# Two dense blocks in one kernel: the first stage's engine work redistributed, one chunk in plain fp32 instead of two

## The reference, cut to what matters

```
mod = silu(c) @ w_ada + b_ada            # a vector times 2048 x 12288
sh1, sc1, ... = split(mod, 6)
h = rmsnorm(x, g_pre_mix) * (1 + sc1) + sh1
proj = h @ w_in                          # 2048 x 11344: qi, qB, kB, vB, kA, vA, qA, ...
```

## Time and profile before

| what | value |
|---|---|
| median of three runs | 2582.1 us (2576.09 to 2584.29) |
| the profiled execution | 2584.16 us, its span 2582.4 us |
| TensorE matmul busy | 2546.8 us, 99% of the span |
| VectorE busy | 1732.4 us, 67% |
| ScalarE busy | 1202.8 us, 47% |
| DMA | 567.11 MB, mean 220 GB/s |
| granted TensorE clock | mean 0.995 of full |
| chain that ended last | PE 89%, DVE 7%, ACT 2%, DMA 1% |

### The profile page before, as it was taken

One profiled execution on the slowest core, in us unless ns is written; L12 is line 12 of the kernel. 1 busy time (PEld: TensorE's weight loads), 2 busy tenths in 40 slices (PEclk: granted clock), 3 DMA queues, 4 the chain that ended last, 5 costly groups with the idle time before them and its releaser, 6 DMA issues.

```text
span 2582.4 us, 30501 instructions
## 1 busy us (share of the span) xinstructions
PE 2546.8 (99%) x12354; PEld 2117.9 (82%) x12354; DVE 1732.4 (67%) x2329; ACT 1202.8 (47%) x1735; POOL 6.4 (0%) x16
## 2 busy tenths in 40 slices
PE   8999999999999999999999999999999999999998
PEld 4787788888887888888888888878788888888887
DVE  6886988788886866556556565546665575664665
ACT  4444445444446434435434465455564344443443
POOL 0000000000000000000000000000000000000000
PEclk9999999999999999999999999999999999999999
DMA  9985276588985785555555545534545555555553
GB/s 399 366 322 186 98 261 264 183 338 313 345 338 221 263 304 192 199 187 187 203 180 192 204 167 180 195 114 147 196 173 200 182 188 203 180 195 196 180 198 145
DMA packets 78748, 567.11 MB, mean 220 GB/s; under 512 B 8800, under 2 KB 8928, under 8 KB 10256
## 3 DMA queue, kind: packets, MB, share of 16 engines
q1 hardware_dynamic: 77472, 558.09, 58.9%
q0 software_dynamic: 1136, 7.07, 0.7%
HBM read 563.02 MB, written 2.10 MB: 219 GB/s over the span
## 4 chain that ended last, share of the span: by engine, by line
PE 89%; DVE 7%; ACT 2%; DMA 1%; issue 1%; DVEq 0%; SPq 0%; ACTq 0%
PE ps L1121 20%; PE ps L1124 20%; PE ps L1122 20%; PE ps L1165 15%; PE ps L1170 8%; DVE wl L1860 3%; DMA raw<-stream_in 1%; DVE ACC L1894 1%; DVE ACC L1881 1%; PE ps L1405 1%; PE ps L1106 1%; ACT wh L1465 1%; PE ps L1381 0%; PE ps L1237 0%; PE ps L1207 0%
## 5 line engine op out<-in xcount | busy, mean ns | idle before, releaser
L1860 DVE TENSOR_TENSOR wl<-raw,wh 128x1024 fp32r<-128x1024 f32 x837 | 986.8, 1220 | 564.3 <-ACT wh L1465 563.9
L1465 ACT ACTIVATE wh<-raw 128x1024 fp32r<-128x1024 f32 x837 | 838.2, 1049 | 715.2 <-PE ps L1124 580.5
L1121 PE MATMUL ps<-wh,U 128*128 128x512 f32 x1376 | 538.8, 392 | 0.0
L1124 PE MATMUL ps<-wl,U 128*128 128x512 f32 x1376 | 537.1, 390 | 1.1 <-DVE wl L1860 1.1
L1122 PE MATMUL ps<-wh,U 128*128 128x512 f32 x1376 | 536.1, 390 | 0.0
L1165 PE MATMUL ps<-HT,wh 128*128 128x512 f32 x1792 | 449.8, 393 | 0.0
L1121 PE MATMUL ps<-wh,HT 128*128 128x512 f32 x1080 | 433.8, 402 | 5.4 <-DVE M L2228 3.4
L1124 PE MATMUL ps<-wl,HT 128*128 128x512 f32 x1080 | 425.4, 394 | 2.4 <-DVE wl L1860 2.3
L1122 PE MATMUL ps<-wh,HT 128*128 128x512 f32 x1080 | 423.8, 392 | 0.0
L1165 PEld LDWEIGHTS ps<-HT,wh 128*128 128x128 f32 x1792 | 323.0, 189 | 58.3 <-DVE M L2265 0.2
L1124 PEld LDWEIGHTS ps<-wl,U 128*128 128x128 f32 x1376 | 258.4, 188 | 58.0 <-DVE wl L1860 4.2
(11 more groups left out here) (284 smaller groups left out, 1473.4 us busy)
## 6 DMA issues: line engine op xcount, KB each, us to landing
raw<-stream_in SPq DMA_DIRECT2D x524, 1024.0 KB, 4.8
M<-rows_in POOLq DMA_DIRECT2D x6, 1024.0 KB, 5.6
M<-stream_in SPq DMA_DIRECT2D x3, 1024.0 KB, 10.9
y_out<-X SPq DMA_DIRECT2D x3, 512.0 KB, 2.6
X<-x_in SPq DMA_DIRECT2D x1, 1024.0 KB, 5.4
X<-x_in SPq DMA_DIRECT2D x2, 512.0 KB, 15.3
raw<-stream_in SPq DMA_DIRECT2D x1, 640.0 KB, 7.2
raw<-stream_in SPq DMA_DIRECT2D x1, 512.0 KB, 3.4
```

The costliest lines, as they stand in the source:

```text
L1121: e.matmul(o, ah, H[:, c:c + bw], start=k == k0, stop=False)
L1124: ins = e.matmul(o, ah, L[:, c:c + bw], start=False, stop=end)
L1465: e.activation(H, raw[place[n][0]][:, c:c + w], ACT.Copy).then_inc(*hi.tick(p))
L1860: e.tensor_tensor(L, raw[place[n][0]][:, c:c + w], H.bitcast(F32), ALU.subtract).then_inc(*lo.tick(p))
```

## The change

1. `PLAIN` holds only the chunk qi@0; qB@0 is split like the rest. (It has blocks 0 and 1 of its slab.)
2. The stream: group 1's four events no longer stand together behind vB@0's first chunk; two come ahead of kB@0 and two behind it. In group 3 the extra event moves from the sixth chunk to the first (vA@0's third). The second 1024 columns of x's last 128 tokens are fetched behind qi@0's transfer and not ahead of it.
3. The head: 24 `constants` come first of all. VectorE takes two events of group 1 before qB@0's banks and two before kB@0's. The split of a chunk stands between the token halves of the chunk before. Group 1's column sum and `xhalves` of blocks 2 and 3 now stand ahead of all four banks of vB@0's first chunk, not ahead of the last one.
4. Group 2 has one accumulator (ACC2 is halved).
5. In `run`, VectorE takes one row block of the "s" events, then one `wl`, and so on in turn. Where a slab has an earlier part and the chunk is its last (kA@1, vB@1, kB@1, qB@1), the rows are put behind the move of bank (1, 0), and the two `wl` come first.

```diff
-PLAIN = ("qi@0", "qB@0")
+PLAIN = (("g", "qi@0", 0),)
...
-    out += group_events(0) + chunks("qi@0") + chunks("qB@0") + chunks("kB@0") + chunks("vB@0", 0, 1) + group_events(1)
+    second = group_events(1)
+    out += group_events(0) + chunks("qi@0") + chunks("qB@0") + second[:2] + chunks("kB@0") + second[2:] + chunks("vB@0", 0, 1)
     beside(chunks("vB@0", 1) + chunks("kA@0") + chunks("vA@0", 0, 2), group_events(2), (1, 2, 2, 2, 1))
-    beside(chunks("vA@0", 2) + chunks("kA@1") + chunks("vB@1") + chunks("kB@1", 0, 1), group_events(3), (1, 1, 1, 1, 1, 2, 1))
+    beside(chunks("vA@0", 2) + chunks("kA@1") + chunks("vB@1") + chunks("kB@1", 0, 1), group_events(3), (2, 1, 1, 1, 1, 1, 1))
...
+                if events[nx][0] == "s":
+                    rows += [(nx, j) for j in range(2)]
+                    if events[nx][2] == 7:
+                        sums.append(nx)
+                else:
+                    sums += ada(nx)
                 nx += 1
+            if rows:
+                late_rows = rows if EARLIER.get(name) and i + 1 == total else []
+                for j in range(2):
+                    split_piece(nx, j, only=("ACT",))
+                lows = [] if hold and own else list(parts[nx])
+                for m, j in () if late_rows else rows:
+                    add("DVE", "ada", m, j)
+                    if lows:
+                        add("DVE", "split", lows.pop(0))
+                for p in lows:
+                    add("DVE", "split", p)
+                if late_rows:
+                    def rest_of_rows(late_rows=late_rows):
+                        for m, j in late_rows:
+                            add("DVE", "ada", m, j)
+                    hooks[1, 0] = rest_of_rows
...
+    def whole(n, between=None):
+
+        name = events[n][1]
+        for t in range(2):
+            for b in range(2):
+                add("bank", name, parts[n], t, b, True, True)
+                evac(name, t, b)
+            if between and t == 0:
+                between()
+        at["done"] = parts[n][-1]
+
+    def chunk(name, i=0):
+        return events.index(("g", name, i))
+
+    add("constants", 24)
     add("xsquare", 0)
...
-    native(5)
+    split(chunk("qB@0"))
     add("xq", 1, 1)
...
-    for n in (5, 6):
-        if n == 6:
-            add("ada", 8)
-            add("ada", 9)
-        split(n + 1)
-        for t in range(2):
-            for b in range(2):
-                add("bank", events[n][1], parts[n], t, b, True, True)
-                evac(events[n][1], t, b)
-        at["done"] = parts[n][-1]
-    for n in (10, 11):
+    second = [events.index(e) for e in group_events(1)]
+    for n in second[:2]:
         add("ada", n)
+    whole(chunk("qB@0"), lambda: split(chunk("kB@0")))
+    for n in second[2:]:
+        add("ada", n)
+    whole(chunk("kB@0"), lambda: split(chunk("vB@0")))
     for j in range(2):
-        split_piece(12, j, only=("ACT",))
+        split_piece(chunk("vB@0", 1), j, only=("ACT",))
+    add("DVE", "split", parts[chunk("vB@0", 1)][0])
+    colsum(second[3])
+    add("xhalves", 1)
+    add("DVE", "split", parts[chunk("vB@0", 1)][1])
+    for t in range(2):
+        add("xq", 2, t)
     for t in range(2):
         for b in range(2):
-            add("bank", "vB@0", parts[7], t, b, True, False)
-            if (t, b) == (1, 0):
-                colsum(11)
-                add("xhalves", 1)
...
-        ACC2 = early.enter_context(nc.sbuf_tensor("ACC2", [128, 1024], F32))
+        ACC2 = early.enter_context(nc.sbuf_tensor("ACC2", [128, 512], F32))
...
-        return [ACC[:, 0:w], ACC2[:, 0:w]] if g in (1, 2) else [ACC[:, 0:256 if g == 0 else w]]
+        return [ACC[:, 0:w], ACC2[:, 0:w]] if g == 1 else [ACC[:, 0:256 if g == 0 else w]]
...
         for n, (off, w) in enumerate(offs):
-            if n == 4:
-                for j in range(2):
-                    a = slice(1024 * j, 1024 * j + 1024)
-                    e.dma_start(X[:, 1, a], x_in[0, 128:256, a]).then_inc(x_landed[1 + j], 16)
+            if n in (4, 5):
+                a = slice(1024 * (n - 4), 1024 * (n - 4) + 1024)
+                e.dma_start(X[:, 1, a], x_in[0, 128:256, a]).then_inc(x_landed[n - 3], 16)
```

More of the change, by code:

```diff
@@ L336, in native @@
             parts[n].append(len(pieces))
-            pieces.append({"n": n, "ks": ks, "width": 1024, "w": 1024, "c": 1024 * (ks[0] - 2 * events[n][2]), "slot": None})
+            pieces.append({"n": n, "ks": ks, "width": 1024, "w": 1024, "c": 1024 * (ks[0] % 2), "slot": None})
     def split(n, room=None):
@@ L398, in run @@
                 split(n + j)
-            nx, sums = n + many, []
+            nx, sums, rows = n + many, [], []
             while nx < len(events) and events[nx][0] != "g":
@@ L405, in run @@
                     sums = []
-                sums += ada(nx)
-                nx += 1
+                if events[nx][0] == "s":
[4 more added lines that the diff above has]
+                    sums += ada(nx)
+                nx += 1
+            if rows:
[14 more added lines that the diff above has]
+                    hooks[1, 0] = rest_of_rows
             if hooks is not tail and hooks is not head:
-                if hold and own:
-                    for j in range(2):
-                        split_piece(nx, j, only=("ACT",))
                 split(nx)
@@ L625, in work_order @@
     add("constants", 4)
-    native(4)
+    native(chunk("qi@0"))
     add("xfloat", 0)
@@ L643, in work_order @@
     at["done"] = parts[4][-1]
-    for n in (5, 6):
-        if n == 6:
-            add("ada", 8)
-            add("ada", 9)
-        split(n + 1)
-        for t in range(2):
-            for b in range(2):
-                add("bank", events[n][1], parts[n], t, b, True, True)
-                evac(events[n][1], t, b)
-        at["done"] = parts[n][-1]
-    for n in (10, 11):
+    second = [events.index(e) for e in group_events(1)]
+    for n in second[:2]:
         add("ada", n)
+    whole(chunk("qB@0"), lambda: split(chunk("kB@0")))
+    for n in second[2:]:
+        add("ada", n)
+    whole(chunk("kB@0"), lambda: split(chunk("vB@0")))
     for j in range(2):
-        split_piece(12, j, only=("ACT",))
+        split_piece(chunk("vB@0", 1), j, only=("ACT",))
[5 more added lines that the diff above has]
+        add("xq", 2, t)
     for t in range(2):
         for b in range(2):
-            add("bank", "vB@0", parts[7], t, b, True, False)
-            if (t, b) == (1, 0):
-                colsum(11)
-                add("xhalves", 1)
[L664 to L669, removed]
+            add("bank", "vB@0", parts[chunk("vB@0")], t, b, True, False)
+    at["done"] = parts[chunk("vB@0")][-1]
+    at["pos"] = chunk("vB@0", 1)
     def third_pair():
@@ L1021, in read_last @@
     def read_last(n):
-        if events[n][1] in PLAIN:
+        if events[n] in PLAIN:
             return gemm(("piece", last_piece[n]))
@@ L1101, in bank_mm @@
                     e.wait_ge(*s(k))
[L1102 to L1110, removed]
+            for p in ps:
+                ks = pieces[p]["ks"]
+                if pieces[p]["slot"] is None:
+                    n, k, c = pieces[p]["n"], ks[0], pieces[p]["c"] + 512 * b
+                    e.wait_ge(*(floated_v if k else floated)(("hf", k, t)))
+                    e.wait_ge(*arrived(n))
+                    ins = e.matmul(o, HF[:, k, 128 * t:128 * t + 128], raw[place[n][0]][:, c:c + 512], start=k == 0,
+                                   stop=last and k == k1 - 1)
+                    keys = [("piece", p)] if (t, b) == (1, 1) else []
+                    if last and k == k1 - 1:
+                        keys.append((name, t, b))
+                    if keys:
+                        ins.then_inc(*gemm.tick(*keys))
+                    continue
                 H, L = piece_memory(p)
-                ks = pieces[p]["ks"]
                 for j, k in enumerate(ks):
@@ L1860, in split, with ada @@
             e.tensor_tensor(L, raw[place[n][0]][:, c:c + w], H.bitcast(F32), ALU.subtract).then_inc(*lo.tick(p))
-        def ada(n):
+        def ada(n, only=None):
             kind, g, i = events[n]
@@ L1870, in ada @@
                 for j, k in enumerate(ks):
+                    if only not in (None, j):
+                        continue
                     a, r = both[k % len(both)], raw[place[n][0]][:, step * j + r0:step * j + r0 + w]
```

## The result

The changed kernel takes 2589.48 us (median of 9, 2587.49 to 2591.05); the kernel before, beside it, 2582.39 (2576.09 to 2586.19). Ratio 1.0028, interval 1.0018 to 1.0037: 7.1 us slower. A second comparison on another chip gave 2589.34 against 2582.52, ratio 1.0025 (1.0016 to 1.0034). The forecast was 2581.7, no change, with a range of 2574 to 2589; the measured time lies 7.8 us above it and just outside the range. The prediction took 0.3% for about the least that can be told. The change is 0.28%, and its interval leaves out 1.

The account below looks back on a forecast made before the run. TensorE was taken to set the pace, with VectorE just keeping up and setting group 2's end. The profiled 2584.2 less 1.5 gave 2582.7; taking off half of the profile's 2.1 above its median gave 2581.7, range 2574 to 2589.

Parts of the forecast that it names:

- rival C: Head: clock falls at the gap before 24.6 or at 44.6, costing 5.1 us; 2587.8 or 2590.9; chance 0.17.
- The two waits of VectorE in group 2: Group 2: taking turns makes wl wait for ScalarE's copy, 0.65 us at 53.3 and 1.15 at 58.8.
- +1.7 us on all that follows: Opening: x's late second part, squared ahead of xfloat, moves the first plain matmul from 22.37 to 24.05.
- a gap of some 2.7 us: Rival C's threshold: the clock falls from a TensorE gap of that length on, as at 80.1.
- +2.75: Group 2: VectorE's last row block ends at 83.5, not at 80.75, that much later.
- One accumulator: Group 2: second row block +0.5 us, dependent neighbours +0.9; the second column sum at half clock saves 1.7.
- Now the late rows pay: Up to 140 us: bank moves of kA@1 and vB@1 come ahead of rows, so the 2.8 us wait goes.
- block 6: After group 2: TensorE, done at 98.6, waits for h's block until 100.0; before 98.1, so +1.9.
- Group 4 has the same order with equal loads; I take nothing for it: Group 4: the new order costs nothing, with 1 us either way.
- rival D: Group 4: late rows put VectorE behind, TensorE waits 1 to 2 us in several chunks; 2585 to 2590; chance 0.08.
- just keeps up: From 170 us on: both engines full, 46 matmuls in 10 us, TensorE sets the pace and VectorE barely follows.
- half clock that comes or stays away: Kernel before: two half-clock stretches cost 5.1 and 3.1 us; without them 2584.2 becomes 2576.0, the fastest run.

Follow-up runs that it names:

- x_float_first_rows_first: Changed kernel with xfloat ahead of the last square of x, and row blocks before both wl where rows are not late: 2581.54 us, ratio 0.9993.
- three_steps_back_cold: three_steps_back without the 24 ones-matmuls at the start: 2576.02 us, ratio 0.9980.
- three_steps_back: Changed kernel with xfloat ahead of the last square of x, rows before both wl, and no late rows: 2577.34 us, ratio 0.9983.
- before_one_accumulator: Kernel before with one accumulator in group 2 and the extra event of group 3 moved to the first place: 2578.34 us, ratio 0.9986.
- one_accumulator_only: Kernel before with one accumulator in group 2 and nothing else: 2579.07 us, ratio 0.9998.
- old_head: Kernel before up to vB@0's second chunk, with the changed run order, one accumulator in group 2 and the moved event: 2585.73 us, ratio 1.0018.
- rows_first: Changed kernel, but VectorE takes all row blocks before both wl where rows are not late: 2585.62 us, ratio 1.0016.
- no_late_rows: Changed kernel, but row blocks are never put behind the bank moves; turns kept: 2585.65 us, ratio 1.0017.
- x_float_first: Changed kernel with the square of x's last part behind xfloat on ScalarE, not ahead of it: 2585.95 us, ratio 1.0015.

## Why the prediction was wrong

Three steps of the sum failed. The half clock in the head was put at nothing and left to rival C; it came as two stretches of 3.4 us, which cost TensorE 1.7 us each. The two waits of VectorE in group 2 were put at 1.8 us and were 4.5. The late rows were put at nothing in group 4 and took 2.7 to 3.0 us there.

**The late x: right in mechanism, the size short.** "+1.7 us on all that follows", 22.9 to 24.6, was 23.49 in this profile and 23.58 to 24.33 in others of the same head; the second part of x landed at 21.9 and not at 22.8. Not in the forecast, but in rival C, was what the gap does: the four records behind it at 2.94 us instead of 1.96, clock 0.83 over 20 to 30 (0.66 in three of the other four). The next gap, the wait and the column sum at 45 to 48, did it again (0.63 us records at 48.95). I had seen both gaps, priced them as a rival of 0.17 and left them out of the sum. Both falls were in all five profiles of the new head with the late x. That is the first step that failed. Nor did it take "a gap of some 2.7 us": 2.08 us were enough. The rule of the Trainium skill that I put there ("TensorE: Matmul & The Clock Gate", "Part 1: The HAM clock gate": the clock falls after idle time) agrees with these rows.

The rows do not say how much idle time is enough, and the same code comes out both ways. The light sum of 1.9 us at 46.97 in the kernel before, without a wait, was followed by no fall, nor in the three other traces with its head. Behind a wait of 0.53 to 0.80 the same sum was followed by one in eight traces and by none in two (x_float_first_rows_first and three_steps_back_cold). Behind the wait of 2.8 us for block 6 the clock fell in three traces and not in three. At column sum 2 it fell in all six traces with a wait of 3.0 to 3.4 us, and in the kernel before with a wait of 0.61 and sums of full length; it fell in none of the seven with a wait of 0.7 and sums of half the length.

**The turns: right in mechanism, mis-sized.** "0.65 us of waiting at 53.3 and 1.15 at 58.8" were 2.25 and 2.29. These 2.7 us more are all but the whole difference between "+2.75" and the measured +5.5. The copy waits for TensorE's ring, and TensorE was 2.1 us later than in my sum: vB@0's first chunk ran from 47.86 to about 55.0 and not from 47.4 to 52.9. Of this, 1.7 us are the half clock at 48 (24 matmuls in 7.2 us, 5.5 at full clock). So the two losses feed each other. With x in time and the rows first there is no wait left in x_float_first_rows_first, and the sum is at 79.96; in three_steps_back, with the same code up to there but a fall of the clock at 45.6, one wait of 0.95 is left and the sum is at 80.57.

**One accumulator: the cost right, the gain undersized.** +1.7 at column sum 2 in before_one_accumulator (+1.35 in one_accumulator_only) against +1.4 in the sum. I gave it 1.7 us back at half clock; that the clock need not fall at all behind sums half as long isn't in the sum. In the changed kernel it fell nevertheless, behind a wait of 3.43.

**"Now the late rows pay" was wrong.** The 2.8 us wait was taken away by moving the event, which leaves one event where two stood ahead of vB@1's bank moves; without late rows it did not come back. Where TensorE is not late, it only changed places with the wait for block 6, 2.8 us in before_one_accumulator, which I had put at 1.4. In the changed kernel TensorE came to block 6 late, out of the half clock, at 101.93, and waited only 0.27. Whether late rows without the moved event would have taken the wait away wasn't run.

**"Group 4 has the same order with equal loads; I take nothing for it" was wrong.** This was rival D. In the kernel before, VectorE is at the rows behind qB@1's banks at 179.01, after at 181.98. Before:

```profile
171.82 2.60 DVE L1881 SCALAR_TENSOR_TENSOR ACC<-raw,VT,ACC 128x1024 f32<-128x1024 f32 x2
174.34 2.35 DVE L1860 TENSOR_TENSOR wl<-raw,wh 128x1024 fp32r<-128x1024 f32 x2
176.61 2.48 DVE L2228 TENSOR_TENSOR M<-ps,M 128x512 f32<-128x512 f32 x4
179.01 2.60 DVE L1881 SCALAR_TENSOR_TENSOR ACC<-raw,VT,ACC 128x1024 f32<-128x1024 f32 x2
```

After:

```profile
150.45 2.36 DVE L1891 TENSOR_TENSOR wl<-raw,wh 128x1024 fp32r<-128x1024 f32 x2 [0.78 <-ACT wh L1496]
...
154.98 0.69 DVE L1984 TENSOR_TENSOR HT<-TMP,HT 128x512 fp32r<-128x512 f32 x1 [0.97 <-ACT HT L1529]
...
174.65 2.36 DVE L1891 TENSOR_TENSOR wl<-raw,wh 128x1024 fp32r<-128x1024 f32 x2 [1.28 <-ACT wh L1496]
176.93 2.02 DVE L2261 TENSOR_TENSOR M<-ps,M 128x512 f32<-128x512 f32 x3
178.86 2.60 DVE L1914 SCALAR_TENSOR_TENSOR ACC<-raw,VT,ACC 128x1024 f32<-128x1024 f32 x2
181.38 0.68 DVE L2261 TENSOR_TENSOR M<-ps,M 128x512 f32<-128x512 f32 x1
181.98 1.27 DVE L1914 SCALAR_TENSOR_TENSOR ACC<-raw,VT,ACC 128x1024 f32<-128x1024 f32 x1
```

The banks themselves are not waited for here. With the rows put behind them, VectorE stands idle three times for ScalarE, 0.78, 0.97 and 1.28 us, where in the kernel before it had rows to do: 3.03 us together, as much as the delay. These three waits are in all four traces with late rows that were read for it (the changed kernel twice, old_head, rows_first), the last at 1.03 to 1.29; in no_late_rows 0.27 of them is left, and none in three_steps_back. It is what the turns do in group 2, once more. The kernel before has VectorE 99% busy at 170 to 180, so there is no room to make 3 us up, and TensorE stops twice for a `wl`, once behind each of kB@1 and qB@1:

```profile
164.10 0.50 PE L1155 MATMUL ps<-wl,HT 128*128 128x512 f32 x1 [1.35 <-DVE wl L1891]
...
186.78 0.50 PE L1155 MATMUL ps<-wl,HT 128*128 128x512 f32 x1 [0.63 <-DVE wl L1891]
```

I had noted that VectorE "just keeps up" there and still took equal loads for equal times.

**The sum.** Forecast for the profiled execution 2582.7, measured 2588.4. Of the 5.7 us, 1.3 were there at column sum 3 (138.05 against 139.32; the kernel before is at 139.42 there, not at 139.58 as I had it), the head's loss being partly caught up by then; 2.7 come from the late rows before column sum 4; 1.6 arise after it. These last are open: from column sum 4 to the end the fourteen traces took 2390.3 to 2393.1 us, with no part of the change that goes with it.

**What the clock is worth.** The prediction read the spread of the kernel before as half clock that comes or stays away. The record bears this out: of its 98 runs beside the experiments, the 7 with a granted clock of 0.999 have a median of 2577.4 us, the 14 with 0.995 one of 2585.5. The same can be set against the changes. An estimate of the time lost to half clock is the span times (1 less the mean granted clock); the clock of each run is recorded to 0.001, so the estimate is good to about 1 us.

| kernel | us above before | mean granted clock | estimated clock loss above before, us |
|---|---|---|---|
| before | 0 | 0.9968 | 0 |
| changed (19 runs) | +7.0 | 0.9954 | +3.7 |
| x_float_first | +4.2 | 0.9960 | +2.0 |
| rows_first | +3.8 | 0.9965 | +0.9 |
| no_late_rows | +3.9 | 0.9951 | +4.4 |
| x_float_first_rows_first | -1.0 | 0.9984 | -4.1 |
| three_steps_back | -4.9 | 0.9975 | -2.0 |
| before_one_accumulator | -4.2 | 0.9981 | -3.4 |

By this estimate about half of the 7.0 us is clock. Most of what the late x and the turns cost is in it, and most of what one accumulator gains; the late rows' 3 us are not.

By runs: late x 2.8, turns 3.1, late rows 3.1 us, each alone out of the changed kernel; all three 11.9. That is more than the 7.0 that the change cost: the 4.9 between are what its other parts gain, and before_one_accumulator, with two of these, lies 4.2 below before.

## What to carry to other kernels

Where an engine takes its work in a fixed order and is nearly full, put work whose inputs have landed ahead of work that waits for another engine: fair turns, or "urgent first", make it idle in front of a late input with ready work behind. A transfer moved back moves back everything that stands behind its reader on that engine, whether it needs the data or not. And price a half clock behind each new gap of the matrix engine into the sum, by how often it came in traces, and not only into a rival.

## What had not been expected

By the estimate above the clock of TensorE decides about half of the result. A wait and column sum of 2.7 us (from 80.1) were followed by 10 us at half clock in the kernel before, and column sums half as long, behind a wait of 0.7, by none in seven traces. And the 24 ones-matmuls at the start did what the opening rows promise, 1.89 us for 8 records instead of 3.57, and brought nothing to the end.
